# First two output tiles of each FFN's last chunk in two parts: three ready channel pairs first, the last pair after

## What is computed

```python
def conv_ffn(h, buf, w_in, w_conv, b_conv, w_out):
    z, new_buf = causal_dwconv(h @ w_in, buf, w_conv, b_conv)
    return (jax.nn.gelu(z[..., :D_FF]) * z[..., D_FF:]) @ w_out, new_buf
# in the trunk, for each of the two layers
    o, fbuf = conv_ffn(h, ...)
    x = x + m[:, 5] * rmsnorm(o, g[3])
```

## Time and profile before

| quantity | value |
|---|---|
| median of 3 runs | 3474.8 us (3472.29 to 3483.05) |
| profiled execution, its own time | 3475.36 us |
| its span in the profile | 3473.6 us |
| TensorE busy with matmuls (PE) | 3152.9 us, 91% of the span |
| VectorE (DVE) | 1717.3 us, 49% |
| GpSimd (POOL) | 1110.1 us, 32% |
| ScalarE (ACT) | 912.8 us, 26% |
| mean granted clock of TensorE | 0.948 of full speed |

### The profile page before, as it was taken

How to read it: one execution, slowest core, us unless ns; L and a number is a source line. 1 busy time by engine, 2 the same in 40 slices (tenths; PEclk the granted TensorE clock), 3 DMA queues, 4 the chain that set the end, 5 groups by cost and what they waited for, 6 DMA issues and landing times.

```text
span 3473.6 us, 55872 instructions
## 1 busy us (share of the span) xinstructions
PE 3152.9 (91%) x22204; PEld 2848.9 (82%) x22204; DVE 1717.3 (49%) x3120; ACT 912.8 (26%) x1454; POOL 1110.1 (32%) x803
## 2 busy tenths in 40 slices
PE   6997889999999986979777999999879999999996
PEld 4886879999999986979644666676769999999996
DVE  3675274445344346541267887701346453453445
ACT  4553131112111023010124777700223021121111
POOL 1322323333333331323013555500323333343341
PEclk9998999999999998989778999999889999999997
DMA  5223132112222122320245000076211111111112
GB/s 197 78 77 115 64 113 81 67 67 79 73 79 73 43 89 86 107 88 31 95 136 176 2 2 3 2 231 211 92 67 54 49 46 46 49 44 48 49 44 106
DMA packets 76438, 274.67 MB, mean 79 GB/s; under 512 B 8698, under 2 KB 19330, under 8 KB 72722
## 3 DMA queue, kind: packets, MB, share of 16 engines
q1 hardware_dynamic: 74226, 255.82, 20.8%
q10 hardware_dynamic: 1984, 15.62, 1.3%
HBM read 247.58 MB, written 33.10 MB: 81 GB/s over the span
## 4 chain that ended last, share of the span: by engine, by line
PE 66%; issue 16%; DVE 9%; DVEq 2%; ACT 2%; DMA 2%; POOL 1%; POOLq 1%; SPq 0%; ACTq 0%
PE PA L1690 30%; PE PB L1690 30%; DVE ring L1051 2%; DVEq L1904 1%; DVE t L1900 1%; DVE ring L1048 1%; DMA mw<-in_mw 1%; DMA mt<-in_mw 1%; PE PC L269 1%; PE PA L956 1%; ACT ring L1020 1%; PE PC L971 1%; PE PC L1746 1%; POOL w_lo L1502 1%; POOL ring L1104 1%
## 5 line engine op out<-in xcount | busy, mean ns | idle before, releaser
L1500 POOL TENSOR_TENSOR w_hi<-w_raw,misc 128x1024 fp32r<-128x1024 f32 x197 | 378.1, 1919 | 1904.9 <-PE PA L1690 738.4
L1502 POOL TENSOR_TENSOR w_lo<-w_raw,w_hi 128x1024 fp32r<-128x1024 f32 x197 | 500.9, 2543 | 28.4 <-issue 0.4
L1690 PE MATMUL PB<-hB_lo,w_hi 128*128 128x344 f32 x1392 | 296.4, 321 | 9.8 <-POOL w_lo L1502 9.8
L1690 PE MATMUL PA<-hB_hi,w_hi 128*128 128x344 f32 x1416 | 302.8, 322 | 2.5 <-POOL w_lo L1502 2.5
L1690 PE MATMUL PA<-hB_lo,w_hi 128*128 128x344 f32 x1416 | 300.9, 321 | 0.0
L421 DVE SCALAR_TENSOR_TENSOR zb<-ub,vec,zb 128x1024 f32<-128x1024 f32 x48 | 155.9, 3247 | 290.6 <-ACT zb L389 290.6
L1690 PE MATMUL PB<-hB_hi,w_hi 128*128 128x344 f32 x1392 | 296.8, 322 | 0.9 <-POOL w_lo L1502 0.9
L1690 PE MATMUL PA<-hB_hi,w_lo 128*128 128x344 f32 x1320 | 279.5, 320 | 0.0
L1690 PE MATMUL PB<-hB_hi,w_lo 128*128 128x344 f32 x1296 | 273.4, 319 | 0.0
L421 DVE SCALAR_TENSOR_TENSOR za<-ua,vec,za 128x1024 f32<-128x1024 f32 x48 | 153.5, 3198 | 204.4 <-ACT za L389 204.4
L1690 PEld LDWEIGHTS PB<-hB_lo,w_hi 128*128 128x128 f32 x1392 | 236.2, 189 | 10.2 <-POOL w_lo L1502 10.2
(11 more groups left out here) (451 smaller groups left out, 6330.0 us busy)
## 6 DMA issues: line engine op xcount, KB each, us to landing
w_raw<-in_w SPq DMA_DIRECT2D x197, 512.0 KB, 3.5
mt<-in_mw SPq DMA_DIRECT2D x48, 1024.0 KB, 5.0
pages<-in_pages SPq DMA_DIRECT2D x64, 384.0 KB, 4.3
x_dram<-X SPq DMA_DIRECT2D x12, 1032.0 KB, 3.9
X<-x_dram SPq DMA_DIRECT2D x3, 4128.0 KB, 12.3
mw<-in_mw SPq DMA_DIRECT2D x4, 2048.0 KB, 22.6
vall<-in_pages_v SPq DMA_DIRECT2D x64, 128.0 KB, 2.5
X<-in_xT SPq DMA_DIRECT2D x4, 1032.0 KB, 8.9
```

Source lines behind the costliest of these rows:

```text
L1500: pool.tensor_tensor(w_hi[b], w_raw[b], zero.broadcast_to([P, 1024]), ALU.add)
L1502: pool.tensor_tensor(w_lo[b], w_raw[b], w_hi[b].bitcast(F32), ALU.subtract).then_inc(sem("w_split"), 1)
L1690: mm = pe.matmul(PS[ps][:, c, 0:CH], w[:, w0:w0 + P], x[:, k, c * CH:(c + 1) * CH], start=(k == 0 and n == 0), stop=(k == K - 1 and n == 2))
```

## The change

The two output tiles of weight tile d = 0 in the last chunk's down are made in two parts. First come the slices of pairs 0, 1 and 2 for b = 0 and b = 1. Then, behind a wait for the last pair, come the slices of pair 3 for b = 0 and b = 1. The new helper `products` issues the 9 matmuls of one slice. The other three weight tiles and all other chunks are as before. This holds for both FFNs.

```diff
+        def products(ws, ps, acts, k, w0, first, last):
+            whi, wlo = w_hi[ws], w_lo[ws]
+            for n, (w, x) in enumerate(((whi, acts[0]), (whi, acts[1]), (wlo, acts[0]))):
+                for c in range(NCH):
+                    mm = pe.matmul(PS[ps][:, c, 0:CH], w[:, w0:w0 + P], x[:, k, c * CH:(c + 1) * CH],
+                                   start=(first and n == 0), stop=(last and n == 2))
+            return mm
...
         def down(c, w, last_chunk=False):
 
-            pe.wait_ge(sem("g_ready"), c * PAIRS + (PAIRS + FT * l))
-            for d in range(4):
+            if last_chunk:
+                pe.wait_ge(sem("w_split"), w + 1)
+                for ks in ((0, 1, 2), (3,)):
+                    pe.wait_ge(sem("g_ready"), c * PAIRS + (ks[-1] + 1 + FT * l))
+                    for b in range(2):
+                        if ks[0] == 0:
+                            pe.wait_ge(sem("ev_act"), c * 8 + (E0 + b + 7))
+                        for k in ks:
+                            mm = products(t0 % 2, (D0 + b) % 2, G, k, k * 256 + b * P, k == 0, k == 3)
+                        if ks[-1] == 3:
+                            mm.then_inc(sem("tile_done"), 1)
+            else:
+                pe.wait_ge(sem("g_ready"), c * PAIRS + (PAIRS + FT * l))
+            for d in range(1 if last_chunk else 0, 4):
                 pe.wait_ge(sem("w_split"), w + d + 1)
                 for b in range(2):
                     if d == 0:
 
-                        pe.wait_ge(sem("ev_act"), c * 8 + (E0 + b + (7 if last_chunk else 9)))
+                        pe.wait_ge(sem("ev_act"), c * 8 + (E0 + b + 9))
                     else:
                         pe.wait_ge(sem("ev_dve"), c * 8 + (V0 + 2 * d + b - 1))
                     tile(None, (t0 + d) % 2, (D0 + b) % 2, G, K=PAIRS, kw=256, off=b * P)
```

## The result

The changed kernel takes 3458.5 us (median of 5 runs, 3458.16 to 3465.74), against 3477.7 us for the kernel before in 5 runs (3472.29 to 3483.05). The ratio is 0.9948, with a 95% interval from 0.9938 to 0.9959. The median fell by 19.2 us. The time lies inside the predicted range, 4.5 us above the predicted time. The profiled execution took 3461.56 us.

The account below looks back on a forecast made before the run. TensorE, busy 91%, was taken to lose time in two 10.8 us waits for `g_lo`. Moved work 16.96 us plus slow clock 5.33 us, less about 1 us, gives 21.3 us: 3475.36 to 3454.1, predicted 3454.0, range 3451 to 3460 us.

Parts of the forecast that it names:

- The likeliest case: Whole kernel: the forecast itself, 21.3 us gained with no clock loss in the short stops, 3452.5 to 3455.5 us, chance 0.62.
- The conditions for an early start: Before the first parts: third pair, weights and b = 0 accumulator ready by 3380.66 us; b = 1 copies at 3382.83 us.
- Second parts, restart and the wait for VectorE: Behind the last g_ready: 18 matmuls (2.83 us), 0.17 us surcharge, small stall; tile d = 1 starts after 3.15 us.
- VectorE's chain beside a busy TensorE: In the stop before the last g_ready: VectorE's chain still lasts 8.46 us, costed at nothing.
- one of my signs of being wrong: In the profile after: VectorE's chain in the last pair is longer than its twin one pair earlier (8.45 us).
- The rival built on it: Last pair: VectorE's chain, stretched beside TensorE to 2.5 times its length, makes the kernel slower, 3479.4 us; chance 0.02.
- the rival in which a wait ahead of the first parts is met late: First parts: b = 1 held leaves 4.2 us on the path per FFN; both held gives 3475 us; chance 0.02.
- What comes behind: Rest of down and norm: nothing uses up the gain; GpSimd's split has 6.9 us to spare, X 36 us.
- The clock in the stop that is left: Stop of 2.3 us per FFN: clock loss taken as nothing, since stops of 2.02 and 2.14 us kept full clock.
- the episode at 1136 us: Among up matmuls: after only 0.95 us of stop the clock was at half for 3.4 us, costing 1.5 us.
- the clock rival: Restart after the short stop: clock falls, costing 1.5 us per FFN, 3455.6 or 3457.1 us, at most 3459.4; chance 0.28.
- The old slow stretch as a fixed term: First down tile after the old stop: slow clock costs 2.97 and 2.36 us, so 5.33 us is gained.

Follow-up runs that it names:

- e2_filled_stop: Changed kernel plus 14 useless matmuls in each FFN between the first and second parts, to fill the short stop: 3456.8 us, ratio 0.9943.
- e9_second_only: The kernel before with the change made in the second FFN alone: 3470.9 us against 3475.4 us, ratio 0.9981.
- e8_two_and_two: Changed kernel with the cut after two pairs, so 36 matmuls lie in the stop and 36 behind it, not 54 and 18: 3466.3 us, ratio 0.9962.

## Why the prediction came out as it did

The direction, the size and the range were right: 3458.5 us in 3451 to 3460 us. The likeliest case was not what happened.

**The conditions for an early start** were right. All 54 matmuls ran from the last up tile on, without a gap, at full clock. One reading was off and changed nothing: the accumulator of b = 0 was not free before the last up tile, but some 2 us into it, when ScalarE's copies ended.

**Second parts, restart and the wait for VectorE.** I predicted 3.15 us from the restart to tile d = 1; with the clock kept it is 3.10 us. The surcharge of the first group is 1282.72 - 1282.14 - 0.47 = 0.11 us (I took 0.17 us). The stop is 2.37 us (2.3 us). With the clock kept, the places gain 10.8 and 10.2 us (30.78 - 19.94 and, by e2_filled_stop, 30.17 - 19.95), where I had 10.95 and 10.35 us.

**VectorE's chain beside a busy TensorE** I costed at nothing; it is 0.06 us longer in each FFN. By the letter this is one of my signs of being wrong, but it is worth 0.1 us of 21.3. In the last pair the chain takes 8.46 us wherever TensorE stands idle beside it (6 places in all profiles) and 8.51 to 8.53 us wherever matmuls run beside it (20 places). The twin one pair earlier takes 8.45 us beside a busy TensorE, so it was a good but not an exact stand-in. The rival built on it, and with it the side "slower", falls. So does the rival in which a wait ahead of the first parts is met late.

**What comes behind** was right. From the third addition on, the distance to the next is 5.65 us as before. `X` and GpSimd's split stayed hidden; no later wait grew.

**The clock in the stop that is left: this step failed.** I wrote "I take nothing, as the stops of like length had nothing". The clock fell at both places of the first profile, and at one of the two in each of the next. The two rows I relied on were a poor sample, and the one episode that spoke against them was the better guide: a stop need not be long to be followed by a slow stretch. The Trainium skill, in "TensorE: Matmul & The Clock Gate", section "A second HAM failure mode: psum-queue depth-cycling", tells of a kernel in which short and frequent pauses between groups of matmuls made the clock go up and down. The trace agrees that short pauses can do it, and goes further: here a single pause of 2.4 us was enough at 5 of 8 places. The price of a loss was 1.3 us where I had 1.5 us from the episode at 1136 us. The sum with both losses is 3454.1 + 2.6 = 3456.7 us, with one 3455.4 us. The rival had 3457.1 and 3455.6 us. The rest of the distance to 3458.5 us has to do with where the sum starts and not with the change: it starts at one execution of 3475.36 us, and the median of before came out at 3477.7 us with more runs. It is also inside what medians of this kernel scatter: its three were 3455.0, 3458.5 and 3460.3 us. That the time stayed in the range is owed to the clock rival, which the range took in.

**The old slow stretch as a fixed term.** I took 2.97 and 2.36 us from one profile. In the second profile of before they are 2.93 and 1.83 us, so the term of the second FFN has a play of at least 0.5 us that my range did not name. Nor was all of it clock: about 0.3 us in each is the last matmul's end and the restart. Against the filled stops (5.98 us) the clock's part is 2.64 + 2.03 = 4.7 us in that profile, not 5.33 us. The gain is not touched by this, as the sum counts these 0.3 us by themselves.

## What to carry to other kernels

When an accumulation waits for its last slice, the slices that are ready can be summed before the wait, over as many accumulators as are free. The gain is the number of matmuls moved times their pitch, and it is only seen if every other wait of the tile (weights, free accumulator) is met by then. Count what is left of the stop as a risk to the clock even if it is short, and fill it with useful work from the next tile where a free bank allows. A gain of under 0.5% in a kernel with idle stretches elsewhere should be read at its place in several profiles, as the rest of the kernel moves by as much.

## What the runs showed of the hardware

- After a stop of 2.4 us, with dense matmuls before and behind it, the granted clock fell to half for 3.4 us at 5 of 8 places. It had fallen by the restart in one case (e9_second_only) and fell up to 1.4 us behind it in the others. The two outcomes at a place differed by 1.3 us and nothing lay between them. At the second FFN it fell 4 times in 4, at the first once in 4.
- Stop and restart together were at half clock for 13.7 or 10.2 us with a stop of 10.8 us, for 6.8 us with one of 5.2 us (e8_two_and_two, both places), and for 3.4 us or not at all with one of 2.4 us.
- The attention stage took 1223 to 1233 us for the same instructions, in step with its mean granted clock (0.82 to 0.64 in a part of 120 us).
- VectorE's chain in the last pair took 8.46 us beside an idle TensorE and 8.52 us beside a busy one, with the 0.06 us in one instruction (L421). The same chain one pair earlier took 8.45 us beside a busy TensorE, so the difference does not hold for every pair. The cause is open.
- Restoring the clock alone, by matmuls without use, made the two places together 4.0 to 4.6 us faster in two profiles and the kernel no faster in 23 runs. The mean clock of these runs rose by 0.0013 where 0.0034 was due, so slow clock came back elsewhere. The cause is open.
